# Query and key heads of a hybrid layer turned by DMA transposes of 16-bit planes, in place of TensorE

## The reference

```python
qm = rms_norm(heads(q_m, MOBA_HEADS), moba_q_gain[l])   # 8 heads of 128, over 256 tokens
km = rms_norm(heads(k_m, MOBA_HEADS), moba_k_gain[l])
# rms_norm: x * rsqrt(mean(x * x) + eps) * gain, along the 128 of a head
s_own = jnp.einsum('bhqd,bhkd->bhqk', q_i, k_own) * scale          # causal, softmax
```

## Time and profile before

| what | value |
|---|---|
| median of three runs | 467.33 us (466.58 to 467.56) |
| the profiled execution | 467.19 us |
| its span, first to last instruction | 465.4 us |
| TensorE busy | 461.0 us, 99% |
| VectorE, ScalarE, GpSimd busy | 304.5, 258.3, 16.8 us |
| granted TensorE clock | 1.0 in the whole span |

### The profile page before, as it was taken

The page is one execution under the profiler, slowest core; times in us unless marked ns, Lnnn a source line. Parts: engine busy times, 40 slices in busy tenths (PEclk is TensorE's granted clock), DMA queues, the critical chain, the costliest instruction groups (busy, mean ns, idle before and its releaser), DMA issues.

```text
span 465.4 us, 7850 instructions
## 1 busy us (share of the span) xinstructions
PE 461.0 (99%) x3133; PEld 425.3 (91%) x3133; DVE 304.5 (65%) x379; ACT 258.3 (55%) x374; POOL 16.8 (4%) x28
## 2 busy tenths in 40 slices
PE   8999999999999999999999999999999999999997
PEld 6899999888888999999999788999999999988886
DVE  4789994845664637345348676787887888884313
ACT  5866353057765849341445355787776667663300
POOL 0100000311110001000000000000000000000000
DMA  8995555263445424754453643626545555548002
GB/s 270 423 417 218 214 206 179 92 214 146 181 143 218 184 91 183 315 182 158 159 205 130 253 149 127 234 69 236 195 185 201 196 197 192 189 140 312 0 1 90
DMA packets 14698, 87.20 MB, mean 187 GB/s; under 512 B 1616, under 2 KB 2512, under 8 KB 5328
## 3 DMA queue, kind: packets, MB, share of 16 engines
q1 hardware_dynamic: 14256, 85.25, 49.1%
q0 software_dynamic: 416, 1.57, 0.9%
HBM read 85.77 MB, written 1.05 MB: 187 GB/s over the span
## 4 chain that ended last, share of the span: by engine, by line
PE 85%; DVE 7%; DMA 4%; ACT 1%; SPq 1%; issue 1%; DVEq 0%; ACTq 0%
PE bank L399 15%; PE bank L400 15%; PE bank L401 15%; PE bank L351 5%; PE bank L352 5%; PE bank L353 5%; DMA w_raw<-weights_dram 4%; PE bank L660 4%; PE bank L658 4%; PE bank L657 4%; DVE w_pair L961 3%; PE bank L420 2%; PE bank L563 2%; PE bank L565 2%; PE bank L564 2%; ACT w_pair L677 1%
## 5 line engine op out<-in xcount | busy, mean ns | idle before, releaser
L961 DVE TENSOR_TENSOR w_pair<-w_raw,w_pair 128x2048 fp32r<-128x2048 f32 x73 | 166.0, 2288 | 82.2 <-ACT w_pair L677 81.9
L677 ACT ACTIVATE w_pair<-w_raw 128x2048 fp32r<-128x2048 f32 x73 | 138.3, 1919 | 30.4 <-PE bank L660 17.1
L399 PE MATMUL bank<-h_hi,w_pair 128*128 128x256 f32 x512 | 143.7, 281 | 0.2 <-DVE w_pair L961 0.2
L400 PE MATMUL bank<-h_lo,w_pair 128*128 128x256 f32 x512 | 142.9, 279 | 0.0
L401 PE MATMUL bank<-h_hi,w_pair 128*128 128x256 f32 x512 | 142.9, 279 | 0.0
L399 PEld LDWEIGHTS bank<-h_hi,w_pair 128*128 128x128 f32 x512 | 96.2, 188 | 0.4 <-DVE w_pair L961 0.4
L400 PEld LDWEIGHTS bank<-h_lo,w_pair 128*128 128x128 f32 x512 | 96.2, 188 | 0.1
L401 PEld LDWEIGHTS bank<-h_hi,w_pair 128*128 128x128 f32 x512 | 96.2, 188 | 0.0
L399 PE MATMUL bank<-a_hi,w_pair 128*128 128x256 f32 x192 | 54.0, 281 | 0.0
L400 PE MATMUL bank<-a_lo,w_pair 128*128 128x256 f32 x192 | 53.6, 279 | 0.0
L401 PE MATMUL bank<-a_hi,w_pair 128*128 128x256 f32 x192 | 53.6, 279 | 0.0
(11 more groups left out here) (143 smaller groups left out, 583.2 us busy)
## 6 DMA issues: line engine op xcount, KB each, us to landing
w_raw<-weights_dram SPq DMA_DIRECT2D x73, 1024.0 KB, 4.9
w_raw<-weights_dram SPq DMA_DIRECT2D x6, 512.0 KB, 8.5
w_raw<-weights_dram SPq DMA_DIRECT2D x4, 256.0 KB, 4.3
ys<-x_dram SPq DMA_DIRECT2D x2, 512.0 KB, 9.6
xs<-x_dram POOLq DMA_DIRECT2D x1, 1024.0 KB, 8.0
area<-decay_dram SPq DMA_DIRECT2D x1, 768.0 KB, 9.9
out_dram<-ys SPq DMA_DIRECT2D x3, 256.0 KB, 2.0
xs<-x_chan_dram SPq DMA_DIRECT2D x1, 512.0 KB, 5.9
```

The costliest lines, as they stand in the source:

```text
L399: mm(o, s_hi, r_hi[:, k, :], start=(k == 0 and m % 2 == 0), stop=False)
L400: mm(o, s_hi, r_lo[:, k, :], start=False, stop=False)
L677: A(w_parts(n, r)[0], raw[r][:, :], ACT.Copy).then_inc(hi_ready, 1)
L961: tt(lo, raw[r][:, :], hi.bitcast(f32), ALU.subtract).then_inc(lo_ready, 1)
```

## The change

VectorE still normalises a block into `qn`. GpSimd then copies the 32-bit values as two planes of 16-bit words (`split_words`, two copies per block, one per 128 tokens). SyncE turns each plane of each head by a DMA transpose of 128x128 words (`turn_heads`, 16 per block, 64 in all), from `planes` to `turned`, which lie in parts of `area` and `ys`. VectorE writes the two planes back as 32-bit values into `qm_t` and `km_t` (`join_words`). The queries get no gain any more; the keys are multiplied by the product of both gains, by ScalarE in place (`scale_keys`). Since `planes` and `turned` exist twice (for queries and for keys), heads 4 to 7 wait until heads 0 to 3 of the same kind were turned and joined. SyncE's loads up to half 27 are written out so that the transposes can stand between them: those of the blocks 0 to 3 behind the loads of halves 21, 23, 25 and 27.

```diff
@@ -142,6 +143,9 @@
         probs = [xs[:, 0:1536].rearrange("p (h s) -> p h s", h=4),
                  ys[:, 0:1536].rearrange("p (h s) -> p h s", h=4)]
         merged = ys[:, :].rearrange("p (k s) -> p k s", k=KT)
+        planes, turned = ([part.bitcast(u16).rearrange(form, t=NT, w=2, h=4) for part in parts] for form, parts in (
+            ("p (t w h c) -> p t w h c", (area[:, 4096:5120], ys[:, 0:1024])),
+            ("p (t w h s) -> p t w h s", (area[:, 5120:6144], ys[:, 1024:2048]))))
 
         bank = [ctx.enter_context(nc.psum_tensor(f"bank{i}", [P, 512], f32)) for i in range(8)]
 
@@ -273,8 +282,24 @@
                     sp.dma_start(decay, decay_in).then_inc(tables_loaded, 16)
                     sp.dma_start(mask[:, :], mask_in).then_inc(tables_loaded, 16)
                     sp.dma_start(col[:, :], cols).then_inc(tables_loaded, 16)
+            def turn_heads(q):
+                for t in range(NT):
+                    sp.wait_ge(planes_ready, 2 * q + t + 1)
+                    if q % 2:
+                        sp.wait_ge(heads_joined, 2 * (q - 1) + t + 1)
+                    for w in range(2):
+                        for h in range(4):
+                            sp.dma_start(turned[q // 2][:, t, w, h, :], planes[q // 2][:, t, w, h, :], transpose=True)\
+                                .then_inc(heads_turned[q % 2][t], 16)
+
             ROUNDS = (HALVES - SLOTS) // SLOTS
-            with sp.Fori(1, ROUNDS) as i:
+            TURN_LAST = 2 * K_M1 + 9
+            for n in range(2 * SLOTS, TURN_LAST + 1):
+                sp.wait_ge(lo_ready, n - SLOTS + 1)
+                sp.dma_start(raw[n % SLOTS][:, :], weights[n]).then_inc(raw_loaded[n % SLOTS], 16)
+                if n >= 2 * Q_M0 + 9 and n % 2:
+                    turn_heads((n - 9) // 2 - Q_M0)
+            with sp.Fori(TURN_LAST // SLOTS, ROUNDS) as i:
                 for r in range(SLOTS):
                     sp.wait_ge(lo_ready, i * SLOTS + (r + 1))
                     sp.dma_start(raw[r][:, :], weights[i * SLOTS + (r + SLOTS)]).then_inc(raw_loaded[r], 16)
@@ -301,6 +326,17 @@
                 step(nc.gpsimd.tensor_scalar(dst, src, factor, EPS, ALU.mult, ALU.add))
                 return nc.gpsimd.tensor_tensor(dst, dst, neg_half[:, 0:width], ALU.pow)
 
+            def split_words(q):
+                for t in range(NT):
+                    wait_bank_read(pool, Q_M0 + q, t)
+                    if q % 2:
+                        pool.wait_ge(heads_turned[0][t], 16 * 8 * (q // 2 + 1))
+                    elif q:
+                        pool.wait_ge(unit_made, unit("ret_t1", 1) + 1)
+                    nc.gpsimd.tensor_copy(planes[q // 2][:, t].rearrange("p w h c -> p w (h c)"),
+                                          qn[:, q % 2, t].bitcast(u16).rearrange("p (c w) -> p w c", w=2))\
+                        .then_inc(planes_ready, 1)
+
             nc.gpsimd.memset(w_parts(SLOTS - 1)[1][:, 0:P].bitcast(f32), 0.0).then_inc(zeros_ready, 1)
             step(nc.gpsimd.memset(neg_half[:, :], -0.5))
             for t in range(NT):
@@ -311,6 +347,9 @@
             for q in range(4):
                 pool.wait_ge(sums_qk, 2 * (q + 1))
                 inv_sqrt(inv_qk[:, q, :], ss_qk[:, q, :], 1.0 / HEAD, 8).then_inc(inv_qk_ready, 1)
+                split_words(q)
+            nc.gpsimd.tensor_tensor(col[:, COL_K_GAIN:COL_K_GAIN + 1], col[:, COL_K_GAIN:COL_K_GAIN + 1],
+                                    col[:, COL_Q_GAIN:COL_Q_GAIN + 1], ALU.mult).then_inc(gains_ready, 1)
 
             pool.wait_ge(unit_made, unit("probs0", 3) + 1)
             pool.dma_start(x_tok, x_view).then_inc(x_again, 16)
@@ -486,8 +520,8 @@
                 for j in range(4):
                     h = 4 * g + j
                     if j == 0:
-                        for which in ("q_m", "k_m"):
-                            wait_unit_read(pe, unit(f"{which}{g}", 1))
+                        pe.wait_ge(heads_joined, 2 * g + 2)
+                        pe.wait_ge(k_scaled, NT * (g + 1))
                     o = start_unit(f"scores{g}", j)
 
                     mm(o[:, 0:P], qm_t[:, h, 0:P], km_t[:, h, 0:P], start=True, stop=False)
@@ -527,15 +561,11 @@
             tail_ret_out()
             token_block(Q_M0)
             token_block(Q_M1)
-            head_transposes("q_m0", Q_M0, qn[:, 0])
             tail_ret_transpose(0)
             token_block(K_M0)
-            head_transposes("q_m1", Q_M1, qn[:, 1])
             tail_ret_transpose(1)
             token_block(K_M1)
-            head_transposes("k_m0", K_M0, qn[:, 0])
             token_block(V_M0)
-            head_transposes("k_m1", K_M1, qn[:, 1])
             token_block(V_M1)
             tail_scores(0)
             channel_block(GATE_R0, h_hi, h_lo)
@@ -728,14 +758,13 @@
                         wait_unit_read(act, unit("inv_row", 0))
                     A(h_hi[:, k, :], hn_t[:, k, :], ACT.Copy).then_inc(h_hi_ready, 1)
 
-            def head_read(name, dst, gain):
-
-                act.wait_ge(tables_loaded, 48)
+            def scale_keys(g):
+
+                act.wait_ge(gains_ready, 1)
                 for t in range(NT):
-                    u = unit(name, t)
-                    act.wait_ge(unit_made, u + 1)
-                    A(dst[:, :, P * t:P * t + P], ubank(u)[:, :].rearrange("p (h s) -> p h s", h=4),
-                      ACT.Identity, scale=col[:, gain:gain + 1]).then_inc(unit_read[u % 4], 1)
+                    act.wait_ge(heads_joined, 2 * (2 + g) + t + 1)
+                    part = km_t[:, 4 * g:4 * g + 4, P * t:P * t + P]
+                    A(part, part, ACT.Identity, scale=col[:, COL_K_GAIN:COL_K_GAIN + 1]).then_inc(k_scaled, 1)
 
             def silu_gates(b):
                 act.wait_ge(half_used, 2 * b + 2)
@@ -833,12 +862,10 @@
                 V_R1: lambda: ret_values_high(V_R1),
                 G_R0: lambda: silu_gates(G_R0), G_R1: lambda: silu_gates(G_R1),
                 Q_M0: lambda: square_heads(Q_M0),
-                Q_M1: lambda: (head_read("q_m0", qm_t[:, 0:4], COL_Q_GAIN), square_heads(Q_M1)),
-                K_M0: lambda: (head_read("q_m1", qm_t[:, 4:8], COL_Q_GAIN), square_heads(K_M0)),
-                K_M1: lambda: (head_read("k_m0", km_t[:, 0:4], COL_K_GAIN), square_heads(K_M1)),
-                V_M0: lambda: (head_read("k_m1", km_t[:, 4:8], COL_K_GAIN),
-                               copy_block(V_M0, lambda t: v_m[:, t, 0:512])),
-                V_M1: lambda: copy_block(V_M1, lambda t: v_m[:, t, 512:1024]),
+                Q_M1: lambda: square_heads(Q_M1), K_M0: lambda: square_heads(K_M0),
+                K_M1: lambda: square_heads(K_M1),
+                V_M0: lambda: (copy_block(V_M0, lambda t: v_m[:, t, 0:512]), scale_keys(0)),
+                V_M1: lambda: (copy_block(V_M1, lambda t: v_m[:, t, 512:1024]), scale_keys(1)),
                 GATE_R0: lambda: exps(1),
                 GATE_R1: lambda: sigmoid_gates(GATE_R1, GATE_R0, 0),
                 RET_O0: lambda: (attn_read(0), probs_read(1)), RET_O1: lambda: attn_read(1),
@@ -1077,12 +1104,19 @@
                 dve.wait_ge(inv_qk_ready, q + 1)
                 if q >= 2:
 
-                    dve.wait_ge(unit_made, unit(f"q_m{q - 2}", 1) + 1)
+                    dve.wait_ge(planes_ready, 2 * (q - 2) + 2)
                 for t in range(NT):
                     tt(qn[:, q % 2, t].rearrange("p (h d) -> p h d", h=4),
                        block_bank(b, t)[:, :].rearrange("p (h d) -> p h d", h=4),
                        inv_qk[:, q, 4 * t:4 * t + 4].unsqueeze(2).broadcast_to([P, 4, HEAD]), ALU.mult)\
                         .then_inc(bank_read[b % 2], 1)
+
+            def join_words(q):
+                for t in range(NT):
+                    dve.wait_ge(heads_turned[q % 2][t], 16 * 8 * (q // 2 + 1))
+                    dst = (qm_t if q < 2 else km_t)[:, 4 * (q % 2):4 * (q % 2) + 4, P * t:P * t + P]
+                    nc.vector.tensor_copy(dst.bitcast(u16).rearrange("p h (s w) -> p w h s", w=2), turned[q // 2][:, t])\
+                        .then_inc(heads_joined, 1)
 
             def ret_gate(g):
                 for j in range(2 * g, 2 * g + 2):
@@ -1214,6 +1248,8 @@
                     split(2 * b + 4)
                 second.get(b, lambda: None)()
                 split(2 * b + 5)
+                if Q_M1 <= b <= V_M0:
+                    join_words(b - Q_M1)
             residual(0, 0)
             residual(0, 1)
             normalise2(0)
```

More of the change, by code:

```diff
@@ L40 @@
 UNITS = {}
-for _name, _count in (("inv_row", 1), ("ret_scores", 4), ("ret_out", 4), ("q_m0", 2), ("ret_t0", 2),
-                      ("q_m1", 2), ("ret_t1", 2), ("k_m0", 2), ("k_m1", 2), ("scores0", 4), ("scores1", 4),
+for _name, _count in (("inv_row", 1), ("ret_scores", 4), ("ret_out", 4), ("ret_t0", 2),
+                      ("ret_t1", 2), ("scores0", 4), ("scores1", 4),
                       ("probs0", 4), ("moba_out0", 2), ("probs1", 4), ("moba_out1", 2), ("h2_t0", 2), ("h2_t1", 2),
```

(6 more changed lines are left out.)

## The result

The changed kernel takes 502.93 us (502.78 to 503.28, four runs) against 467.23 us in the same runs: ratio 1.0768, interval 1.0755 to 1.078. The forecast was 463.8 us.

What follows compares the result with a forecast made beforehand. TensorE's instruction list was taken as the bound, busy 99% of the span. 467.19 - 3.5 for removed transposes + 0 for hidden additions = 463.7, or 463.8 with the runs' median 0.14 higher; range 462.8 to 465.5 us.

Steps and rivals of the forecast that it cites:

- X: Time from one DMA transpose to the next on SyncE's queue; taken as 0.6 us, limit for staying hidden 0.75.
- Rival (a): SyncE's queue: transposes follow each other in 0.8 to 1.3 us, making the kernel slower than before; chance 0.23.
- Its formula: Time when SyncE's queue is late: 467.2 - 3.5 + 1.8 + 64(X - 0.75), breaking even at X = 0.78.
- 6 us for reusing words: Blocks 1 and 3 wait for a landing and a join before reusing words, 3 us twice.
- 1.8 us for a split behind the scaling: ScalarE: the split for the next half stands behind the key scaling, adding 1.8 us beyond X = 0.75.
- Its start near 103: GpSimd's first copy ready at about 103: normalised at 99.1, then held by the split at 99.66.
- What is removed: TensorE: four groups of eight head transposes go, 0.88 us each, 3.5 us in all.
- The cover: Added GpSimd, SyncE and VectorE work stays hidden, cost 0; joins 1.15 us, copies 2 us, keys needed by 162.1.
- (b): DMA transposes run one at a time, each a whole landing of 1.8 us: 532.7 us; chance 0.11.
- (c): GpSimd's copies are late, deciding above 3.3 us a copy; 485 us at 6 us a copy; chance 0.07.
- (d): VectorE splits wait up to 4 us for GpSimd copies, stalling 3 us in all: 466.8; chance 0.09 with (e) and ties.
- T: Time of one GpSimd copy of 128x1024 words; taken as 2 us, covered up to 3.3 us.

Runs made afterwards that it cites:

- e3: Changed kernel with `transpose=True` dropped, so the 64 DMAs copy instead of turning: 465.42 us (one run).
- e4: Changed kernel with 64 DMA transposes of 64x128 words in place of 128x128, each half joined twice: 501.2 us (one run).
- e2: Changed kernel with four heads grouped, 16 DMA transposes of 128x512 in place of 64 of 128x128: 463.42 us, ratio 0.9922 to the kernel before.
- e1: Changed kernel with the same words turned by 8 DMA transposes of 128x1024 in place of 64: 463.35 us, ratio 0.9917 to the kernel before.
- e11: Changed kernel with the first four heads' softmax ahead of the last join, plus 96 filling matmuls in TensorE's waits: 494.84 us, ratio 1.0592.
- e8: e1 with the 32 head transposes put back on TensorE, results unused: 467.18 us, ratio 1.0006 to the kernel before.
- e9: Changed kernel with 96 matmuls of 512 columns, results overwritten, filling TensorE's four waits: 503.42 us, ratio 1.0771 to the kernel before.

## Why the prediction was wrong

- **The step that failed is X.** The prediction took 0.6 us for a DMA transpose, "the row of issues behind one another, because the engines behind the queue look cheap". The traces show 1.27 to 1.33 us, with the engines indeed cheap (11 to 13% busy). The reasoning weighed bytes and free engines; what counts is how long an issue of this kind holds SyncE. A plain DMA's issue is 0.60 us (e3), this one's 1.23 whether it turns 64 or 128 rows (e4), 1.29 with 512 columns (e2), and 1.24 with 1024 columns as long as none of that size is ahead of it (e1).
- **Rival (a) is what happened**, with its place and its sign. Its formula gives 501 us at X = 1.30 and 502.93 was measured, but part of that fit is luck. It charged 6 us for reusing words, which never showed (the join is done when the queue is), so the keys were ready at 192.4 and not at 114.4 + 64 x 1.30 = 197.6. It also charged 1.8 us for a split behind the scaling, which e11 does not show. It left out the softmax behind the last join (6.0 us), the clock (2.1 us) and the loads between the runs of transposes (3.7 us). Its start near 103 is right for another reason: the first copy was ready at 100.5, and the transposes stood behind the load of half 21, which was issued at 102.65.
- **The figure of the Trainium skill.** The Trainium skill ("VectorE: DVE Perf Modes", The three transpose paths) has 1309 ns for one 128x128 transpose. The trace agrees in size, 1.27 to 1.33 us from one to the next. I gave a price near it less weight than a row of another kind of DMA. But it is not a price per tile: e2 turned four such tiles in one instruction for 1.29 us.
- **What is removed: right.** 3.5 us forecast; putting the transposes back in e8 costs 3.83 us (467.18 - 463.35; the two were measured on different chips, and by their ratios to the kernel before it is 4.2 us).
- **The cover: right, with room.** Joins 0.75 us and not 1.15, GpSimd copies 1.5 us in the mean and not 2; e1's scores 1 at 161.95 against 162.1. With the queue free, the forecast time of 463.8 is met by e1 at 463.35.
- **Rivals (b), (c) and (d).** The transposes do not run one at a time: one starts every 1.3 us and lands after 2.4. GpSimd's T stayed under 3.3 us. A split that fell on a running GpSimd copy grew by 0.44 to 0.86 us, less than the 4 us allowed in (d), and in e1 stalled nothing.

## What to carry to other kernels

Up to 128x512 words a DMA transpose is priced by the instruction on its queue, so turn in one what lies together: the same change with 8 or 16 transposes in place of 64 is 0.8% faster than the kernel before and 7.9% faster than the change as made. Free DMA engines say nothing about a queue; before work is put on it, its issues have to be multiplied by a row of the same kind. Where there is none, the sign of the change has to be worked out over the whole range between the nearest rows, here 0.33 to 1.8 us with the break-even at 0.78. When one late item is placed in an in-order list, what is queued behind it (here a softmax that did not need it) is late too, after the chain itself has ended.

## What the runs showed of the hardware

- A DMA transpose of 16-bit words holds the issuing queue for some 1.2 to 1.3 us, whether it turns 64x128, 128x128 or 128x512 words (medians 1.23, 1.23 and 1.29 us), and for 1.24 to 1.47 us with 128x1024 words and no other of that size ahead of it. A second one of 128x1024 right behind the first holds it for 3.4 to 4.4 us. A plain DMA of 32 KB takes 0.60 us in a row. The transposes of 32 KB land 2.4 us after their issue in the median, those of 256 KB 6.2 us (5.4 to 7.9).
- GpSimd's copies and VectorE's splits and joins took turns: the one that started first kept its time, and the other was held until it ended. In the changed kernel a copy takes 1.04 us when it starts first, and the split that begins 0.22 us behind it takes 2.96 in place of 2.29. A copy that starts 0.09 us behind a join (0.76 us) takes 1.56; the split behind that join takes 3.15, and GpSimd's 0.20 us instruction that meets this split takes 2.11 and ends with it:

```profile
114.34 1.04 POOL L336 COPY area<-xs 128x1024 uint16<-128x1024 uint16 x1 [6.81 <-DMA area<-area]
125.28 1.56 POOL L336 COPY area<-xs 128x1024 uint16<-128x1024 uint16 x1 [9.91 <-DMA area<-area]
126.93 2.11 POOL L326 TENSOR_SCALAR inv_qk<-ss_qk 128x8 f32<-128x8 f32 x1
...
114.56 2.96 DVE L988 TENSOR_TENSOR w_pair<-w_raw,w_pair 128x2048 fp32r<-128x2048 f32 x1 [1.12 <-ACT w_pair L707]
125.19 0.76 DVE L1118 COPY area<-area 128x1024 uint16<-128x1024 uint16 x1 [7.00 <-DMA area<-area]
125.84 3.15 DVE L988 TENSOR_TENSOR w_pair<-w_raw,w_pair 128x2048 fp32r<-128x2048 f32 x1
```

- After each of the four long waits (5.1 to 8.1 us) TensorE's granted clock averaged 0.78 to 0.88 over the next 12 to 14 us. In e9 it stayed at 1.00 behind the two waits before V_M0 and V_M1 and behind the last one, which were filled to within 0.9 us; behind the wait before the first scores, of which 3.4 us were left, it averaged 0.75. The lower clock was worth 2.1 us, and only once TensorE was the bound behind it.
